# Expert rows of a retrieval layer gathered once for both products, on one core

## What is computed

```
h = RMSNorm(x)
x = x + W_out[ RMSNorm(MLA(h)) || RMSNorm(ShortConv(h)) ]
x = x + PEER(RMSNorm(x))
y = RMSNorm(x)
```

```
g = softmax(best)
a = gelu(u[expert] . h)
out = sum over the 128 experts of (g * a) * v[expert]
```

## Time and profile before

| | |
|---|---|
| median of three runs | 3739.96 us (3724.41 to 3740.37) |
| profiled execution, span from first to last instruction | 3800.9 us |
| time of the profiled execution around the span | not given |
| mean granted TensorE clock | 0.951 |
| TensorE, VectorE, ScalarE, GpSimd busy | 3167.7, 2264.1, 1732.4, 2342.3 us |
| moved by DMA | 1273.73 MB, mean 335 GB/s |

### The profile page before, as it was taken

The page is one execution under the profiler, slowest core; times in us unless marked ns, Lnnn a source line. Parts: engine busy times, 40 slices in busy tenths (PEclk is TensorE's granted clock), DMA queues, the critical chain, the costliest instruction groups (busy, mean ns, idle before and its releaser), DMA issues.

```text
span 3800.9 us, 49151 instructions
## 1 busy us (share of the span) xinstructions
PE 3167.7 (83%) x12280; PEld 1786.7 (47%) x12280; DVE 2264.1 (60%) x5815; ACT 1732.4 (46%) x4369; POOL 2342.3 (62%) x2127
## 2 busy tenths in 40 slices
PE   7779988898779987899778987799878997788876
PEld 6445444554436544454445544465444544464431
DVE  2774568554674557655684547745575556835674
ACT  2344634454443644445444544445444454436433
POOL 1466755666566765667556765667656676646556
PEclk9899999999899998999899998999989999999989
DMA  5799999999899998999899999999999999979988
GB/s 205 272 357 339 347 346 358 355 351 324 316 376 353 331 351 325 359 364 332 329 365 345 345 325 340 355 366 336 335 329 360 347 345 337 355 262 329 324 291 324
DMA packets 354518, 1273.73 MB, mean 335 GB/s; under 512 B 42944, under 2 KB 44512, under 8 KB 354208
## 3 DMA queue, kind: packets, MB, share of 16 engines
q0 software_dynamic: 304128, 1107.43, 79.7%
q1 hardware_dynamic: 50080, 162.83, 11.6%
HBM read 1264.00 MB, written 5.55 MB: 334 GB/s over the span
## 4 chain that ended last, share of the span: by engine, by line
PE 34%; DVE 20%; issue 19%; DMA 15%; ACT 6%; POOL 3%; another core or an unknown queue 2%; DVEq 1%; SPq 0%; POOLq 0%; ACTq 0%
PE acc L785 20%; DVE ring_u L1241 5%; DMA ring_v<-in_peer_v,idx_peer 4%; DMA wst<-in_w_blocks 4%; DMA ring_u<-in_peer_u,idx_peer 4%; PE Sps L571 4%; PE M L555 2%; DVE bufA L1015 2%; PE Sps L709 1%; ACT L946 1%; PE Sps L608 1%; POOL ring_u L500 1%; POOL ring_v L500 1%; DVE bufA L1206 1%
## 5 line engine op out<-in xcount | busy, mean ns | idle before, releaser
L785 PE MATMUL acc<-ring_v,diag 128*128 128x512 f32 (+1 forms) x4224 | 2108.4, 630 | 540.0 <-ACT diag L813 279.0
L1241 DVE CUSTOM_DVE_ANT_0 ring_u<-ring_u,hf_peer 128x1024 f32<-128x1024 f32 x1024 | 1240.6, 1221 | 519.9 <-DMA ring_u<-in_peer_u,idx_peer 472.5
L785 PEld LDWEIGHTS acc<-ring_v,diag 128*128 128x128 f32 (+1 forms) x4224 | 763.3, 196 | 1476.4 <-issue 1043.6
L500 POOL DMA_INDIRECT ring_v<-in_peer_v,idx_peer x896 | 998.8, 1115 | 642.0 <-PE acc L785 285.5
L500 POOL DMA_INDIRECT ring_u<-in_peer_u,idx_peer x896 | 994.4, 1110 | 417.1 <-issue 247.1
L946 ACT ACTIVATE dots<-dots 128x1 f32<-128x1 f32 x1056 | 210.7, 200 | 977.6 <-DVE dots L1241 748.2
L813 ACT ACTIVATE diag<-ident,dots 128x128 f32<-128x128 f32 x1024 | 411.3, 402 | 458.6 <-PE acc L785 332.0
L813 ACT ACTIVATE dots<-dots,gate_peer 128x1 f32<-128x1 f32 x1024 | 301.4, 294 | 33.2
L500 POOL DMA_INDIRECT ring_u<-in_peer_u,idx_lead x128 | 134.6, 1051 | 290.1 <-DVE dots L1241 120.4
L770 PEld LDWEIGHTS M<-actT,wst 128*128 128x128 f32 x2304 | 286.9, 199 | 42.9 <-issue 40.3
L770 PE MATMUL M<-actT,wst 128*128 128x128 f32 (+1 forms) x2304 | 290.4, 281 | 2.5 <-DMA wst<-in_w_blocks 1.8
(11 more groups left out here) (179 smaller groups left out, 2675.9 us busy)
## 6 DMA issues: line engine op xcount, KB each, us to landing
wst<-in_w_blocks SPq DMA_DIRECT2D x270, 512.0 KB
ring_u<-in_peer_u,idx_peer POOLq DMA_INDIRECT x896
ring_v<-in_peer_v,idx_peer POOLq DMA_INDIRECT x896
x_front<-in_x_p SPq DMA_DIRECT2D x8, 512.0 KB
w_out_sb<-in_w_out SPq DMA_DIRECT2D x8, 512.0 KB, 5.7
o_y_p<-qT SPq DMA_DIRECT2D x8, 512.0 KB
ring_u<-in_peer_u,idx_lead POOLq DMA_INDIRECT x128
ring_v<-in_peer_v,idx_lead POOLq DMA_INDIRECT x128
```

Source lines behind the costliest of these rows:

```text
L500: pool.indirect_dma_start(ring[k % RING][:, :], None, table, bass.IndirectOffsetOnAxis(ap=src[:, k:k + 1], axis=0)).then_inc(sem[k % RING] ...
L785: mm = pe.matmul(acc[0:rows, half * 512:(half + 1) * 512], diag[:, (k % 2) * P:(k % 2) * P + rows], ring_v[k % RING][:, half * 512:(half + ...
L1241: dve.tensor_tensor_reduce(u, u, hf[:, :], 1.0, 0.0, ALU.mult, ALU.add, dots[:, k:k + 1]).then_inc(s_dot, 1)
```

## The change

- One table `peer_uv` holds u and v of an expert in one row of 8 KB, and one gather per slot brings 128 such rows into one of six buffers `ring` of 1 MB. VectorE reads columns 0 to 1023, TensorE the rest. A gather waits until the matmuls of the slot six before are done.
- `x_peer` is gone. TensorE multiplies x_front by the identity into `acc` at the start of a tile (`take_x`), and the slots add to it; VectorE then only copies `acc` to `y_buf`. TensorE gives the semaphore s_handx that ScalarE's copy gave.
- ScalarE squares y in two halves, VectorE adds the two sums at slot 2, and ScalarE takes the root at slot 3.
- To make room, only block 4 of the weights is kept; blocks 2 and 3 are streamed for every tile (32 blocks rather than 30). The scratch for GpSimd's descriptors is halved.
- The loop over tiles is written out on every engine.

```diff
-KEPT = (2, 3, 4)
+KEPT = (4,)
-RING = 4
+RING = 6
...
-        ring_u = [sb(f"ring_u{i}", D) for i in range(RING)]
-        ring_v = [sb(f"ring_v{i}", D) for i in range(RING)]
+        ring = [sb(f"ring{i}", 2 * D) for i in range(RING)]
-        x_peer = sb("x_peer", D)
...
-            with sp.Fori(1, TILES - 1) as t:
+            for t in range(1, TILES):
                 body(t)
-            body(TILES - 1)
...
             def gathers(tile, before, n):
-                for k in range(n + 1):
-                    if k < n:
-                        if k % TOPK == 0 and not sample(tile):
-                            wait_apart(pool, s_idx, PH * tile + k // TOPK + 1)
-                        if not first(tile) or k >= RING:
-                            wait_apart(pool, s_dot, before + k - RING + 1)
-                        gather(ring_u, a["peer_u"], s_gu, tile, k)
-                    if k >= 1:
-                        wait_apart(pool, s_slot, before + k)
-                        gather(ring_v, a["peer_v"], s_gv, tile, k - 1)
+                for k in range(n):
+                    if k % TOPK == 0 and not sample(tile):
+                        wait_apart(pool, s_idx, PH * tile + k // TOPK + 1)
+                    g = before + k
+                    if g >= RING:
+                        wait_apart(pool, s_slot, g - RING + 1)
+                    src = idx_pack if sample(tile) else idx_lead if k < LEAD else idx_peer
+                    pool.indirect_dma_start(ring[g % RING][:, :], None, a["peer_uv"],
+                                            bass.IndirectOffsetOnAxis(ap=src[:, k:k + 1], axis=0)
+                                            ).then_inc(s_g[g % RING], 16)
...
+            def take_x(t):
+                rows = tokens(t)
+                pe.wait_ge(s_xm, 2 * t + 2)
+                if not first(t):
+                    pe.wait_ge(s_x2, t)
+                for half in range(2):
+                    mm = pe.matmul(acc[0:rows, half * 512:(half + 1) * 512], ident[0:rows, 0:rows],
+                                   x_front[0:rows, half * 512:(half + 1) * 512], start=True, stop=False)
+                mm.then_inc(s_handx, 1)
...
             def slot(t, k, n, rows):
-                pe.wait_ge(s_diag, SLOTS * t + k + 1)
-                pe.wait_ge(s_gv[k % RING], 16 * ((SLOTS // RING) * t + k // RING + 1))
+                g = SLOTS * t + k
+                pe.wait_ge(s_diag, g + 1)
+                pe.wait_ge(s_g[g % RING], 16 * (g // RING + 1))
                 for half in range(2):
                     mm = pe.matmul(acc[0:rows, half * 512:(half + 1) * 512], diag[:, (k % 2) * P:(k % 2) * P + rows],
-                                   ring_v[k % RING][:, half * 512:(half + 1) * 512],
-                                   start=(k == 0), stop=(k == n - 1))
+                                   ring[g % RING][:, D + half * 512:D + (half + 1) * 512],
+                                   start=False, stop=(k == n - 1))
...
-                act.wait_ge(s_slot, before + k + RING - 1)
+                if before + k >= 2:
+                    act.wait_ge(s_slot, before + k - 1)
...
             def finish(t):
                 act.wait_ge(s_x2, t + 1)
                 act_y.start(t)
-                root(y_buf[:, :], D, SS2, act_y, x_peer[:, :]).then_inc(s_ss2, 1)
+                act_y.link(act, act.activation(convT[:, :], y_buf[:, 0:512], ACT.Square, accum_out=col(SS2)))
+                act.activation(convT[:, :], y_buf[:, 512:1024], ACT.Square, accum_out=col(SS2B)).then_inc(s_sq2, 1)
+                act_y.end()
+            def finish_root(t):
+                act.wait_ge(s_ss2, t + 1)
+                act.activation(col(SS2), col(SS2), ACT.Sqrt, bias=col(EPSC), scale=1.0 / D).then_inc(s_rt2, 1)
...
-                dve.tensor_tensor(y_buf[rows, :], x_peer[rows, :], acc[rows, :], ALU.add).then_inc(s_x2, 1)
+                dve.tensor_copy(y_buf[rows, :], acc[rows, :]).then_inc(s_x2, 1)
...
+            def sum_squares(t):
+                dve.wait_ge(s_sq2, t + 1)
+                dve.tensor_tensor(col(SS2), col(SS2), col(SS2B), ALU.add).then_inc(s_ss2, 1)
...
-        "peer_u": v["peer_u"][0],
-        "peer_v": v["peer_v"][0],
+        "peer_uv": np.concatenate([v["peer_u"][0], v["peer_v"][0]], axis=1),
...
-                   dynamic_dma_scratch_size=8192)
+                   dynamic_dma_scratch_size=4096)
```

More of the change, by code:

```diff
@@ L247, in build @@
         s_yst = sem("s_y_stored")
-        s_gu = [sem(f"s_u_gathered{i}") for i in range(RING)]
-        s_gv = [sem(f"s_v_gathered{i}") for i in range(RING)]
+        s_g = [sem(f"s_gathered{i}") for i in range(RING)]
         s_init = sem("s_init")
@@ L316, in build @@
         s_x2 = sem("s_x2")
+        s_sq2 = sem("s_y_squares")
+        s_rt2 = sem("s_y_root")
         s_ss2 = sem("s_ss2")
@@ L358, in build @@
         Mb = [M0, M1]
-        SSX, RX, SSQ, RQ, SSK, RK, RC, SSA, RA, SSM, RM, SS2, R2, SSC, EPSC = range(15)
+        SSX, RX, SSQ, RQ, SSK, RK, RC, SSA, RA, SSM, RM, SS2, SS2B, R2, SSC, EPSC = range(16)
         def col(c):
@@ L496, in _ @@
             pool.memset(vv[:, :], 0.0).then_inc(s_init, 1)
[L498 to L502, removed]
-            def gathers(tile, before, n):
-                for k in range(n + 1):
-                    if k < n:
-                        if k % TOPK == 0 and not sample(tile):
-                            wait_apart(pool, s_idx, PH * tile + k // TOPK + 1)
-                        if not first(tile) or k >= RING:
-                            wait_apart(pool, s_dot, before + k - RING + 1)
-                        gather(ring_u, a["peer_u"], s_gu, tile, k)
-                    if k >= 1:
-                        wait_apart(pool, s_slot, before + k)
-                        gather(ring_v, a["peer_v"], s_gv, tile, k - 1)
-            gathers(0, 0, SLOTS)
-            with pool.Fori(1, TILES - 1) as t:
+            def gathers(tile, before, n):
+                for k in range(n):
[8 more added lines that the diff above has]
+                                            ).then_inc(s_g[g % RING], 16)
+            for t in range(TILES):
                 gathers(t, SLOTS * t, SLOTS)
-            gathers(TILES - 1, SLOTS * (TILES - 1), SLOTS)
             pool.wait_ge(s_pack, 16 * 3 * PACK)
@@ L801, in _ @@
             body(0)
-            with pe.Fori(1, TILES - 1) as t:
+            for t in range(1, TILES):
                 body(t)
-            body(TILES - 1)
-            pe.wait_ge(s_x2, TILES)
+            take_x(S_TILE)
             for k in range(PSLOTS):
@@ L932, in front @@
                                        accum_out=gsum[:, h:h + 1]).then_inc(s_ge, 1)
[L934 to L939, removed]
             def slot(t, before, k, gates, eye, rows):
@@ L961, in body @@
                         slot(t, SLOTS * t, k, gate_peer, ident[:, :], P)
[L962 to L965, removed]
+                    if k == 1 and not first(t):
+                        finish(t - 1)
+                    if k == 3 and not first(t):
+                        finish_root(t - 1)
                     if k >= LAG:
@@ L973, in _ @@
             body(0)
-            with act.Fori(1, TILES - 1) as t:
+            for t in range(1, TILES):
                 body(t)
-            body(TILES - 1)
             act.wait_ge(s_pack, 16 * 3 * PACK)
@@ L983, in _ @@
                     finish(TILES - 1)
-                    hand_x(S_TILE)
+                if k == 3:
+                    finish_root(TILES - 1)
             finish(S_TILE)
+            finish_root(S_TILE)
         @block.vector
@@ L1237, in slot @@
             def slot(t, k, hf):
-                dve.wait_ge(s_gu[k % RING], 16 * ((SLOTS // RING) * t + k // RING + 1))
-                u = ring_u[k % RING][:, :]
+                g = SLOTS * t + k
+                dve.wait_ge(s_g[g % RING], 16 * (g // RING + 1))
+                u = ring[g % RING][:, 0:D]
                 dve.tensor_tensor_reduce(u, u, hf[:, :], 1.0, 0.0, ALU.mult, ALU.add,
@@ L1271, in body @@
                         add_experts(t - 1)
+                    if k == 2 and not first(t):
+                        sum_squares(t - 1)
                     if k == 4 and not first(t):
@@ L1284, in _ @@
             body(0)
-            with dve.Fori(1, TILES - 1) as t:
+            for t in range(1, TILES):
                 body(t)
-            body(TILES - 1)
             dve.wait_ge(s_pack, 16 * 3 * PACK)
@@ L1292, in _ @@
                     add_experts(TILES - 1)
+                if k == 2:
+                    sum_squares(TILES - 1)
                 if k == 4:
@@ L1295, in _ @@
             add_experts(S_TILE)
+            sum_squares(S_TILE)
             finish(S_TILE)
```

9 lines of the change are left out of this document (3 added, 6 removed).

## The result

The changed kernel takes 3678.81 us, median of four runs (3673.75 to 3686.27), against 3734.09 us for the kernel before beside it: ratio 0.985, 95% interval 0.9803 to 0.9897. In a later session the same two kernels gave 3688.31 and 3783.67 us, ratio 0.9747 (0.9722 to 0.9772). The level of the kernel before moved by 50 us between sessions (medians 3734, 3782, 3784, 3732 us; the last three were taken on three different chips), that of the changed one by 10 us in the two sessions that ran it. So times are compared within a session, or between the two whose level is the same (3782 and 3784 us). Whether the chip or something else moves the level, and why it moves one kernel more than the other, stays open.

The account below looks back on a forecast made before the run. Transfer engines, 91.3% taken and mostly by gathers, were the nearest thing to a bound, though not the only one. 3800.9 - 75 - 64 - 30 + 20 + 15 + 5 + 20 + 1 = 3693 us, on the median 3634; range 3490 to 3760 us.

Parts of the forecast that it names:

- Point 1: Expert gathers: one gather of 8 KB rows for two of 4 KB takes 3.5% less per byte; 75 us saved.
- Point 2: Gather buffers: 6 MB in flight instead of 4 MB fills part of the transfer engines' idle time; 64 us saved.
- Point 3: Tile loop written out: five looped turns each cost 7 us more; 35 us at most, 30 us taken as saved.
- Points 4 to 6: Losses: x by identity matmul 20 us, two more streamed weight blocks 15 and 5 us, later weight loads 20 us.
- Point 7: GpSimd: 1056 fewer gather instructions, some 1170 us of its work, leaving it busy near 1200 us; no time gained.
- Attention: Stage of slots 62 to 100 of a tile, paced by TensorE: to stay within 3 us of 123 us.
- The identity matmuls: Start of each tile, on TensorE just after s_x2: nine groups of 1.9 to 3.4 us each.
- The own-query stage: Slots 4 to 34 of a tile, paced by transfers and VectorE: to fall from 101 to about 96 us.
- The transfers' share: Transfer engines inside the tiles: a share of 0.95 or more beside a shorter tile, as sign of the deeper ring.
- TensorE's waits for wst: TensorE waiting for streamed weights: from 87 us to about 110 to 130 us; 200 us or more would favour D.
- C: Transfers: bytes alone count, so 8 KB rows give nothing and the ring 0 to 64 us; middle 3740 us, chance 0.14.
- D: Input and query blocks: streamed weights come late behind 8 KB rows, a slower kernel; middle 3820 us, chance 0.18.

Follow-up runs that it names:

- e5: The changed kernel run again, unchanged, with six pairs: 3688.31 us, ratio 0.9747 to the kernel before.
- e1: The kernel before run again, unchanged, with a second profile: 3781.33 us, ratio 0.9995.
- e8: The changed kernel with five pairs instead of six and three kept weight blocks instead of one: 3770.15 us, ratio 0.9972 to the kernel before.
- e7: The changed kernel with six pairs, but u and v gathered by two transfers of 4 KB rows: 3742.89 us, ratio 0.9885 to the kernel before.
- e2: The kernel before with only the tile loop written out: 3747.6 us, ratio 0.9898.
- e3: e2 with one gather of 8 KB rows per slot into four pairs, freed by the matmuls: 4047.78 us, ratio 1.0675 to the kernel before.
- e6: The changed kernel with five pairs instead of six: 3792.78 us, ratio 1.0017 to the kernel before.
- e4: The changed kernel with four pairs instead of six: 4081.16 us, ratio 1.0762 to the kernel before.
- e9: e6 with x_peer, ScalarE's copy and VectorE's add put back: 3784.68 us, ratio 1.0139 to the kernel before.
- e10: e6 with four buffers for streamed weights instead of two: 3727.49 us, ratio 0.9996 to the kernel before.

## Why the prediction was right, and where it was not

The forecast was 3634 us, 2.8% less, in a range of 3490 to 3760 us. 1.5% was measured beside it, and 2.5% in the session of e5. The direction and the range held. The size is about half of the forecast in the first session and near it in the other, and that it came near is in part luck, since the errors of the parts offset each other. Step by step, in the sessions of e1 to e8:

- **Point 1, rows of 8 KB**: taken as 3.5% of the gathers' engine time and 75 us. Measured 3.5% between e7 and e5, at six pairs, and nothing between e2 and e3, at four (3016 and 3014 us). So the 3.5% are no property of the row alone. The 55 us of e7 hold GpSimd's second gather too. Whether the factor of 0.7 for what reaches the end was too high cannot be said; at most 55 of 105 us did.
- **Point 2, the ring**: taken as a plain gain of 64 us from 4 MB to 6 MB. This is the step that failed in its working. It took the megabytes in flight, and left out what the release by the matmuls does to u. At equal depth the merge costs 300 us (e3); the fifth and sixth pair give back 288 and 104 us (e6, e5). Net of rows, e2 plus the 33 us of x and blocks (a price taken at four pairs) is 3781 us and e7 is 3743: the ring gives 38 us. "13.8 us covered by four, 20.7 by six" counted slots and did not ask how long one pair's passage is. The page of the changed kernel shows the landing alone at 8.2 us after issue (median):

```profile
ring<-in_peer_uv,idx_peer POOLq DMA_INDIRECT x896, 8.2
```

Behind it come the dot product, Gelu, the diagonal and the matmuls, each in its queue. Four pairs at 471 us a tile last 4 x 3.68 = 14.7 us and were all in passage, which took 14.2 us from issue to matmuls (e4). At the 3.45 us a slot of the prediction four pairs cover 13.8 us, less than even this shortest passage. "Covered by six" did not end it either: at six pairs the passage is 19.3 us and the ring still full.
- **Point 3, the loop**: taken as 30, measured 34 us (e2). The waits sat at the looped turns and are gone, which agrees with the Trainium skill ("Runtime: NRT & Kernel Launch", section Instruction fetch mechanics).
- **Points 4 to 6, x, two blocks, later weights**: taken as 61 us with the last microsecond; measured together 33 us (e4 less e3), at four pairs. Apart: two blocks 23 us at five pairs (e8) for 20 taken and part of the 20 for lateness; x some 10 us in the turn, at most 29 by the whole tile (e9), for 20. The x matmuls lie on the path, as said. The working priced their slow case at 3.2 us from eight matmuls in 6.35 us, of which the last two ran at 593 to 647 ns; four at the slow rate of 1060 to 1190 ns take 3.75 us, as measured. Against that, they take over the slow stretch that slots 0 and 1 had (6.35 us, now 4.08), which the working missed.
- **Point 7, GpSimd**: 1166.2 us busy, near 1200, as said. That this gives nothing is not shown: e7 takes back GpSimd's saving together with the rows.

The terms as measured are -55 - 38 - 34 + 33 = -94 us, and e5 is 95 us below the kernel before. In the forecast they were -108. That the measured terms meet the total checks nothing: they are the differences e5 less e7, e7 less e2 and the 33 us, e2 less before, and the 33 us again, so the 33 us cancel and the sum is e5 less before by construction. Three terms are below the forecast's (55 or less for 75, 38 for 64, 33 lost for 61), two of them gains and one a loss, so they nearly cancel. The first session, where the kernel before was at 3734 us, gave 55 us. What makes the kernel before 50 us faster there is open, and the prediction had no row for it.

Of the **signs**, three failed and one is open. Attention was to stay within 3 us. It fell by 6 in the first pair of traces, TensorE busy for 112.09 of 118 us, but by 1.4 between e1 and e5, and no more than 1 from e2 to e5; so how far TensorE bounds that stage stays open. The identity matmuls were to take 1.9 to 3.4 us, and took 3.75. The own-query stage was to fall to 96 us and fell to 99.6, VectorE busy for 89.23 of 100 us. The transfers' share was to rise to 0.95; it stayed near 0.93 to 0.94 by tile, at 360 to 362 GB/s instead of 342 to 349. TensorE's waits for wst were put at 110 to 130 us and are 129.0:

```profile
  DMA wst<-in_w_blocks: 129.0, 79
```

The **rivals**. C, that bytes alone count, fell: the packets halved, q0's time fell from 3029 to 2872 us, and 401 GB/s stand in 13 us of the tile; the limit near 358 GB/s that the Trainium skill gives ("DMA: Bandwidth & Descriptors", section Where 436 GB/s comes from) did not bind in it. D named the late weights as what could turn the sign, with "the ring gives nothing" beside it. The lateness exists (129 us of waits, and e10) but not in D's size, 200 us or more. The way to slower that did exist was the merge at too small a depth: at four pairs it is 8.0% slower than e2, and with the loop's gain in it still 6.75% slower than the kernel before. The depth of six is what keeps the sign, and at five the change gives nothing (1.0017).

## What to carry to other kernels

When two transfers are merged, the earlier of the two buffers is held as long as the later one; compare the buffers' time of passage (issue, landing, every consumer's queue) with depth times pace before counting the cheaper transfer as a gain. If depth times pace is less than the passage, the ring sets the pace: at four pairs that cost 300 us here, and at six the ring was still full. And price what the memory could do otherwise: here 8 KB a partition was worth 104 us as a sixth pair and 23 us as kept weights.

## What the runs showed of the hardware that I had not expected

- With six pairs in the ring, gathers of random 8 KB rows took 3.5% less engine time for the same bytes than 4 KB rows (2878 and 2983 us); with four they took the same (3014 and 3016 us). For the same packets the engine time fell from 2998 to 2920 and 2878 us with four, five and six pairs. One stretch of 13 us ran at 401 GB/s.
- The same program moved by 50 us between sessions and chips (3732 to 3784 us), while another that does the same work with half the gathers moved by 10 us in two sessions (3679 and 3688 us).
- A back-edge of the five engines' loops cost 6 to 7 us of TensorE's time at each turn (at one turn 13.48 us of waiting with it, 7.51 us without; the end of a tile 60.3 and 54.7 us).
